# Sample attention's last rounds: cached values of tiles 0 and 1 first, the new values' products at the end

## What is computed

```
k_all = jnp.concatenate([k_past, k_s], axis=1)      # 256 cached + 4 new
v_all = jnp.concatenate([v_past, v_s], axis=1)
c_all = jnp.cumsum(jnp.concatenate([logf_past, logf_s], axis=1), axis=1)
s = einsum('bqhd,bkhd->bhqk', q, k_all) / 8 + (c_new - c_all);  causal mask
o = einsum('bhqk,bkhd->bqhd', softmax(s), v_all)
```

## Time and profile before

| What | Value |
|---|---|
| median of three runs | 2330.48 us |
| the profiled execution's time | 2329.15 us |
| its span, first to last instruction | 2327.3 us |
| TensorE busy | 2282.0 us (98%) |
| VectorE, ScalarE, GpSimd busy | 1031.1, 576.9, 613.1 us |
| mean granted TensorE clock | 0.995 of 2.4 GHz |
| TensorE idle before the first weighted sum | 4.30 us |

### The profile page before, as it was taken

How to read it: one execution, slowest core, us unless ns; L and a number is a source line. 1 busy time by engine, 2 the same in 40 slices (tenths; PEclk the granted TensorE clock), 3 DMA queues, 4 the chain that set the end, 5 groups by cost and what they waited for, 6 DMA issues and landing times.

```text
span 2327.3 us, 36318 instructions
## 1 busy us (share of the span) xinstructions
PE 2282.0 (98%) x14220; PEld 2092.5 (90%) x14220; DVE 1031.1 (44%) x1755; ACT 576.9 (25%) x1264; POOL 613.1 (26%) x439
## 2 busy tenths in 40 slices
PE   7999999999999999999989999999999999999999
PEld 7999999999999967777766666899999999999999
DVE  7842332433323756442136777534433423324332
ACT  5420110110101433332126666422100101101101
POOL 6122222222233612100000110353222222222240
PEclk9999999999999999999989999999999999999999
DMA  4111111111111124444554544111111111111112
GB/s 151 32 50 51 46 46 46 46 46 46 46 46 46 59 74 152 139 133 147 177 165 97 133 114 110 32 46 45 46 49 50 48 47 46 46 46 46 46 55 75
DMA packets 195560, 169.96 MB, mean 73 GB/s; under 512 B 28784, under 2 KB 169120, under 8 KB 195399
## 3 DMA queue, kind: packets, MB, share of 16 engines
q1 hardware_dynamic: 155657, 142.03, 20.8%
q10 hardware_dynamic: 39750, 25.69, 3.6%
HBM read 137.55 MB, written 30.50 MB: 72 GB/s over the span
## 4 chain that ended last, share of the span: by engine, by line
PE 90%; DVE 7%; issue 2%; ACT 1%; DMA 0%; SPq 0%; DVEq 0%; ACTq 0%
PE ps L363 35%; PE ps L616 28%; PE ps L791 13%; PE ps L1490 2%; PE ps L1514 2%; PE ps L490 2%; DVE stat L1576 2%; PE ps L1476 1%; PE ps L1475 1%; PE ps L1265 1%; PE ps L1290 1%; ACT pT L1560 1%; PE ps L807 1%; PE ps L1755 1%; PE ps L1245 1%
## 5 line engine op out<-in xcount | busy, mean ns | idle before, releaser
L363 PE MATMUL ps<-xn_hi,w_lo 128*128 128x352 f32 x1536 | 497.1, 324 | 5.0 <-DVE h L690 3.2
L363 PE MATMUL ps<-xn_lo,w_hi 128*128 128x352 f32 x1536 | 492.4, 321 | 0.0
L363 PE MATMUL ps<-xn_hi,w_hi 128*128 128x352 f32 x1536 | 492.3, 321 | 0.0
L616 PE MATMUL ps<-hid_hi,w_lo 128*128 128x352 f32 x1440 | 464.5, 323 | 0.0
L616 PE MATMUL ps<-hid_lo,w_hi 128*128 128x352 f32 x1440 | 461.9, 321 | 0.0
L616 PE MATMUL ps<-hid_hi,w_hi 128*128 128x352 f32 x1440 | 461.4, 320 | 0.0
L330 POOL CAST w_hi<-w_raw 128x1024 fp32r<-128x1024 f32 x132 | 139.0, 1053 | 1003.4 <-issue 516.7
L690 DVE TENSOR_TENSOR h<-ps,h 128x352 f32<-128x352 f32 x360 | 185.6, 521 | 413.3 <-PE ps L616 413.3
L655 ACT ACTIVATE tmp_b<-tmp_a 128x352 f32<-128x352 f32 x192 | 95.1, 499 | 1092.1 <-DVE tmp_a L673 1092.1
L332 POOL TENSOR_TENSOR w_lo<-w_raw,w_hi 128x1024 fp32r<-128x1024 f32 x132 | 318.8, 2415 | 10.6
L363 PEld LDWEIGHTS ps<-xn_hi,w_lo 128*128 128x128 f32 x1536 | 288.1, 188 | 7.3 <-DVE h L690 4.3
(11 more groups left out here) (243 smaller groups left out, 2729.9 us busy)
## 6 DMA issues: line engine op xcount, KB each, us to landing
w_raw<-in_w_up SPq DMA_DIRECT2D x64, 512.0 KB, 3.9
w_raw<-in_w_down SPq DMA_DIRECT2D x60, 512.0 KB, 3.3
out<-tok_out ACTq DMA_DIRECT2D x32, 256.0 KB, 2.1
qk_dram<-turn_hi ACTq DMA_DIRECT2D x32, 256.0 KB, 2.4
qk_dram<-turn_lo ACTq DMA_DIRECT2D x32, 256.0 KB, 2.9
k_page<-in_cache_k SPq DMA_DIRECT2D x32, 256.0 KB, 3.2
v_page<-in_cache_v SPq DMA_DIRECT2D x16, 512.0 KB, 9.5
q_a<-qk_dram SPq DMA_DIRECT2D x32, 256.0 KB
```

Of the source, the lines that this page charges most:

```text
L363: last = pe.matmul(ps[:, bank, 0:CH], w, x(k, c), start=(k == 0 and i == 0), stop=(k == nk - 1 and i == 2))
L616: last = pe.matmul(ps[:, NC * (dm % 2) + c, 0:CH], w, x, start=(k == 0 and i == 0), stop=(k == GT - 1 and i == 2))
```

## The change

`weigh_sample` is split. `weigh_part` issues the chosen groups of all four blocks; `weigh_cached` waits for the cached values and probabilities and issues the groups on `v_page`; `weigh_own` waits for `v_new` (`s_in`) and issues the groups on it. At the end of sample attention the order becomes: cached sums of tile 0, last scores, cached sums of tile 1, new values' products of tile 0, then of tile 1, and the transposes as before. In ScalarE's stream the exponential of tile 3 comes ahead of the copy of tile 0's sums. The first-matmul flag is set only in the first block of a tile (once for each of the four partition groups of the bank), because the four blocks share one bank and their accumulations now stay open together; the flag of the last matmul is set only in the last block. Tiles 2 and 3 keep `weigh_sample`, now made of `weigh_part`.

```diff
-        def weigh_sample(pe, u, bank):
-
-            pe.wait_ge(s_vg[u], 64)
-            pe.wait_ge(p_ev, 2 * (u + 1))
-            pe.wait_ge(s_in, 16)
+        def weigh_part(pe, u, bank, groups):
+
             for b2 in range(2):
                 for rd in range(2):
                     rows = slice(64 * b2 + 32 * rd, 64 * b2 + 32 * rd + 32)
                     out = slice((2 * b2 + rd) * P, (2 * b2 + rd + 1) * P)
-                    for g in range(3):
+                    for g in groups:
                         for j in range(4):
                             cols = slice((4 * rd + j) * P, (4 * rd + j + 1) * P)
                             x = pT_s[u][:, g, rows] if g < 2 else pTn[u][:, rows]
                             v = v_page[2 * u + b2][g][:, cols] if g < 2 else v_new[:, cols]
-                            last = pe.matmul(ps[32 * j:32 * j + 32, bank, out], x, v, start=(g == 0), stop=(g == 2))
-            last.then_inc(s_pv, 1)
+                            last = pe.matmul(ps[32 * j:32 * j + 32, bank, out], x, v, start=(g == 0 and b2 == 0 and rd == 0),
+                                             stop=(g == 2 and b2 == 1 and rd == 1))
+            return last
+
+        def weigh_cached(pe, u, bank):
+            pe.wait_ge(s_vg[u], 64)
+            pe.wait_ge(p_ev, 2 * (u + 1))
+            weigh_part(pe, u, bank, (0, 1))
+
+        def weigh_own(pe, u, bank):
+            pe.wait_ge(s_in, 16)
+            weigh_part(pe, u, bank, (2,)).then_inc(s_pv, 1)
+
+        def weigh_sample(pe, u, bank):
+            pe.wait_ge(s_vg[u], 64)
+            pe.wait_ge(p_ev, 2 * (u + 1))
+            pe.wait_ge(s_in, 16)
+            weigh_part(pe, u, bank, (0, 1, 2)).then_inc(s_pv, 1)
...
         def sample_pe_end(pe):
             pe.wait_ge(p_ev, 6)
-            weigh_sample(pe, 0, O_BANK[0])
+            weigh_cached(pe, 0, O_BANK[0])
             scores(pe, 7)
             pe.wait_ge(v_ev, 16)
-            weigh_sample(pe, 1, O_BANK[1])
+            weigh_cached(pe, 1, O_BANK[1])
+            weigh_own(pe, 0, O_BANK[0])
+            weigh_own(pe, 1, O_BANK[1])
             turn_sample(pe, 0, O_BANK[0])
             turn_probs(pe, 3)
             turn_sample(pe, 1, O_BANK[1])
...
         def sample_act_end(act):
             act.wait_ge(s_sc, 8)
+            sample_exp(act, 3)
             keep_sample(act, 0)
-            sample_exp(act, 3)
             keep_sample(act, 1)
```

More of the change, by code:

```diff
@@ L1274, in turn_probs @@
             pe.transpose(ps[0:S, bank, 2 * P:3 * P], p_s[:, 2 * P:NKEY], ident[:, :]).then_inc(p_tr, 1)
+        def weigh_part(pe, u, bank, groups):
+            for b2 in range(2):
+                for rd in range(2):
+                    rows = slice(64 * b2 + 32 * rd, 64 * b2 + 32 * rd + 32)
+                    out = slice((2 * b2 + rd) * P, (2 * b2 + rd + 1) * P)
+                    for g in groups:
+                        for j in range(4):
+                            cols = slice((4 * rd + j) * P, (4 * rd + j + 1) * P)
+                            x = pT_s[u][:, g, rows] if g < 2 else pTn[u][:, rows]
+                            v = v_page[2 * u + b2][g][:, cols] if g < 2 else v_new[:, cols]
+                            last = pe.matmul(ps[32 * j:32 * j + 32, bank, out], x, v, start=(g == 0 and b2 == 0 and rd == 0),
[8 more added lines that the diff above has]
+            weigh_part(pe, u, bank, (2,)).then_inc(s_pv, 1)
         def weigh_sample(pe, u, bank):
```

## The result

The changed kernel takes 2335.58 us (median of 18 runs, 2332.24 to 2337.73), the kernel before 2330.49 us (18 runs, 2329.03 to 2332.54) beside it. The ratio is 1.0020, 95% interval 1.0012 to 1.0027: slower by about 5 us, where 8 us faster had been forecast.

What follows compares the result with a forecast made beforehand. TensorE was taken as the bound, 98% busy, with a 4.30 us gap on the path. 8.35 us gained at the prompt start less 0.5 for the clock is 7.85, from the 2330.48 median to 2322.6 us; range 2320.6 to 2325.6.

Steps and rivals of the forecast that it cites:

- Behind it everything hangs on semaphores of earlier work and shifts as a whole: After the third head's first score, all later work was to move earlier with the gain, 7.85 us after the clock term.
- Nothing is added or removed: End of sample attention: the same matmuls are issued, with those reading `v_new` (32 of 96 records per tile) moved last.
- My case on the other side: Clock at 0.50 from about 1189 through the first two heads; up to 2334.5 us at 30 us of it; chance 0.03.
- my signs of being wrong: Transfer holding prompt start beyond 1203.5, 0.50 over more than 8 us after 1199, or the shift gone at the projection.
- The gap and the narrow work: End of sample attention: 4.30 us idle and low clock behind it go; TensorE alone reaches the first prompt score 8.75 us earlier.
- the margin that I gave: `v_new` lands at about 1192.35, 2.25 us after issue, over 2 us before its products need it.
- The first head's transfers: Ahead of prompt attention: issue times unmoved, landing between 1199.0 and 1201.7, taken as 1199.8, so the gain is 8.35 us.
- Rival 2: First head's transfers hold prompt start to 1201.7, plus low first rounds; gain 4.85 us at worst, 2324 to 2325.6; chance 0.12.
- The clock: Prompt attention's first rounds: a low-clock stretch near them was priced at 0.5 us lost, making 8.35 into 7.85.
- rival 3: Long low-clock stretch of 10.24 us on the prompt's first rounds; gain 5.0 to 5.9 us, 2324.6 to 2325.5; chance 0.10.
- Hidden edits: Sample attention's end: ScalarE's exponential moved ahead and accumulation groups left open cost nothing; 0.5 us kept slow-side for the groups.
- the third head's transfers: Prompt attention: queue end stays about 1227.0, first score moves to 1228.5; margin shrinks from 9.9 to 1.5 us but stays.

Runs made afterwards that it cites:

- a_pad2: The changed kernel with two already satisfied waits added to TensorE's stream, ahead of the new values' products of tiles 0 and 1; 2325.85 us, ratio to before 0.9982.
- a_small0: a_pad2 with the first head's six large transfers cut to 128 of 1024 columns, the rest zeroed, so one output is wrong; 2321.45 us, ratio 0.9958.
- a_pad1: The changed kernel with one already satisfied wait added to TensorE's stream, ahead of tile 0's new-value products; 2324.34 us, ratio 0.9976.
- a_actold: a_pad2 with ScalarE's order of before: copy of tile 0's sums, then tile 3's exponential; 2325.39 us, ratio 0.9978.
- a_split3f: a_pad2 with three of the first head's seven transfers issued early and two useless matmuls in the wait for `v_new`; 2322.20 us, ratio 0.9964.
- a_early: a_pad2 with all first-head transfers issued by SP right behind the last V step, and `v_new` issued by ScalarE; 2330.56 us, ratio 1.0002.
- a_fill: a_pad2 with eight useless 128x512 matmuls in the idle gap ahead of the prompt attention; 2326.35 us, ratio 0.9981.

## Why the prediction was wrong

**The step that failed** is the sentence "Behind it everything hangs on semaphores of earlier work and shifts as a whole", together with "Nothing is added or removed". The same matmuls are issued, but two wait instructions went, everything behind them in TensorE's program moved up by two places, and the second MLP, which I had priced at nothing new, took 11.0 us more. The reading that fits the runs: the loop's top slipped over the border of a piece of code (16 KB each: 1.95 MB over 119 packets), so that at each repeat the jump brings in a piece of which almost nothing is left, and the next one has to be fetched before TensorE can go on. The instruction queue shows the extra piece; the changed kernel from 1894 to 1905, and then a_pad2 from 1890 to 1901, the same stretch of work:

```profile
q8 instruction: 3, 0.05, 2.1%
```

```profile
q8 instruction: 2, 0.03, 1.3%
```

The second repeat reads the same: 3 packets from 2083 to 2094 in the changed kernel, 2 from 2074 to 2085 in a_pad2. One piece more at each of two repeats is the 121 against 119. The price: 4.28 + 4.38 us idle less the 0.72 + 0.73 of before is 7.2 us, and the gaps brought the low clock behind them:

```profile
1901.00:1904.40 3.40, 3.40 (x13) 3.40 (x14) 0.00 (x0) 0.00 (x0) 2.66 (x2) 0.55 0.02 5
...
2090.20:2095.60 5.40, 5.40 (x20) 5.40 (x21) 0.00 (x0) 0.00 (x0) 3.40 (x2) 0.54 0.01 3
```

At these means, 3.4 us lost 1.5 and 5.4 lost 2.5, 4.0 together, and 7.2 + 4.0 = 11.2 against the 11.02 of the table. That the number of instructions ahead of the loop is the cause is shown by three runs (two back, one back, two removed without any reordering). That it works by a border between pieces is read from the packet counts and the step between one and two instructions; that it is the loop's top and not its end that crosses the border is argued from the extra fetch at the jump, and not tested.

The forecast for the profiled execution was 2321.3 us and it took 2336.77, 15.5 more. By the four marks, 11.0 of it is this step, 3.0 is the gain up to the projection (4.87 us in place of 7.85, below), and 1.5 the scatter ahead of the key transposes.

None of the five cases had this in it. My case on the other side was a clock low over two heads; the clock was low there for 10.2 us only. The weight on "slower", 0.04, rested on that case alone. Of my signs of being wrong, two showed (the start at 1203.51, by a hair and with the key transposes 1.55 us later; 10.2 us at 0.50), and the third did not: the projection still started 3.3 us earlier. None of them looked behind the projection, where the loss was.

**The gap and the narrow work: right, and under-counted.** Cached sums started 1.0 us behind the last key transposes, at clock 1.00, and the last scores followed as forecast. The block costs were too high. 64 records on cached values took 1.78 us (1189.66 to 1191.44) where I had 2.32, and both tiles' new-value products 1.88 (1195.25 to 1197.13) where I had 2.78: blocks of one kind in a row are faster than the mixed ones of the earlier trace rows. By TensorE alone the start would be 10.6 us behind the key transposes (11.13 less the wait of 0.54 in a_small0), 1.7 less than my 12.3.

**`v_new`: not the margin that I gave.** It landed 3.6 us after its issue in place of 2.25, at 1195.2, just as its products came up; I had over 2 us to spare. In a_pad1 it took 3.9 us and its products waited 0.24.

**The first head's transfers: the right mechanism, a term too small.** I took the landing at 12.7 us behind the key transposes, from the queue's byte count; measured were 14.87 in the changed kernel, 14.1 to 14.2 in a_pad2 and a_pad1, and 13.19 in a_actold. I had these transfers issued at the same times as before. The last of them was issued 7.30 us behind the key transposes before and 7.98 in the changed kernel, where issuing the two `q_a` took 1.81 us in place of 1.14; it was counted 6.64 us later. And the byte count was no good sign of landing. In the changed kernel the queue had moved 1.74 MB by 1201.0, more than this head and `v_new` together (1.71), and yet the last transfer was counted only at 1203.26. The Trainium skill, "DMA: Bandwidth & Descriptors", under "Why a DMA increments its semaphore by 16 and not by 1", says that the engines of a transfer finish independently and are counted one by one; that would explain it, and no run here shows the engines apart. The gain here was 6.2 us in the changed kernel and 7.0 in a_pad2, in place of 8.35. Rival 2 had the mechanism.

**The clock: under-priced.** I took 0.5 us for the first rounds; the projection column has 1.3 to 1.7 more than before with 10.2 us of low clock. This is rival 3's length at less than its price. The idle gap had only changed places, and the low clock behind it changed places too; that the idle time brings it is argued from the fillers, not isolated. Part 4 (PE-mode transpose) of the Trainium skill's "TensorE: Matmul & The Clock Gate", by which transposes don't count toward the full clock, would have the tail bring the fall by itself: in a_small0, with 0.54 us of waiting and the same tail, 0.50 came only behind the first rounds, as before, so the tail alone did not bring it here. With eight fillers that are plain matmuls it did not fall at all; with four, and with two in a_split3f, it fell for 6.8 and 3.4 us.

**Hidden edits: right.** ScalarE's order (a_actold), the groups left open (no run takes them alone) and the third head's transfers cost nothing that shows; there is no wait on the third head's data.

Without the code placement the forecast's sign stands, and 4.5 to 6.0 us of its 7.85: 2324.3 to 2325.9 (a_pad1, a_pad2) against the 2322.6 forecast, 0.2% to 0.3% under the kernel before.

## What to carry to other kernels

A change in one stream moves every later instruction of that stream: where a long loop stands behind it, compare the number of executed instructions and of code packets first, and put one or two satisfied waits in (or take them out) before judging the change. When a wait is removed, list what the stretch behind it waits for with its landing, and don't take a queue's byte count for a landing: here the same 4.3 us of idling stood 11 us further on, with a low clock behind it. Sharing the queue between two things needed soon is a matter of order and bytes, not of which engine issues them; with three transfers early and four late the first score came 12.3 us behind the key transposes, against 14.1 with all late and 19.4 with all early, though the median came clear of that of all late only once the remaining wait was filled.

## What the runs showed of the hardware

- Two redundant wait instructions more or fewer in TensorE's stream are worth 10 us in this kernel (2340.57 against 2330.34; 2325.85 against 2335.58), in a step and not by degrees: one instruction fewer than before had no effect, and 32 more brought no gap.
- A transfer of 128 KB, on ScalarE's queue, took 8.0 us to land while another queue moved 1.50 MB (a_early); issued ahead of the first head's bytes it took 2.2 us before and 2.9 to 3.9 in the kernels with the new order.
- A granted clock of 0.50 over 10.2 us at the prompt attention's start, part of it in idle time, goes with 2.1 to 2.4 us more than the 276.15 of a_fill, one over 3.4 us with 0.6 to 0.75. Useless matmuls in the idle time bought this back: with eight of them the start was 3.0 us later and the time the same within 0.5 us.
- What makes the clock fall for 3.4, 6.8 or 10.2 us after short waits is not settled: four fillers left 6.8 us of it and eight left none.
